# Scatter stage of a PEER encoder layer: one-hot tables made by wide instructions with eight tokens innermost

## The reference, cut to what matters

```
best, sel = lax.top_k(cand, PEER_TOPK)
idx = jnp.take_along_axis(cand_idx, sel, axis=-1)     # first key * 128 + second key
g = jax.nn.softmax(best, axis=-1).astype(h.dtype)
...
a = jax.nn.gelu(jnp.einsum('td,ted->te', xb, u)) * gb
return jnp.einsum('te,ted->td', a, exp_v[ib])
```

## Time and profile before

| what | value |
|---|---|
| median of three timed runs | 5582.73 us |
| profiled execution, its own time | 5577.84 us |
| its span, first to last instruction | 5576.1 us |
| PE / DVE / ACT / POOL busy over the span | 86% / 59% / 26% / 3% |
| mean granted TensorE clock | 0.919 of full speed |
| L1760 + L1761 + L1762 busy | 253.8 + 317.5 + 334.3 us, 1024 instructions each |

### The profile page before, as it was taken

The page is one execution under the profiler, slowest core; times in us unless marked ns, Lnnn a source line. Parts: engine busy times, 40 slices in busy tenths (PEclk is TensorE's granted clock), DMA queues, the critical chain, the costliest instruction groups (busy, mean ns, idle before and its releaser), DMA issues. The chain is left out here.

```text
span 5576.1 us, 62426 instructions
## 1 busy us (share of the span) xinstructions
PE 4798.6 (86%) x21520; PEld 3810.7 (68%) x21520; DVE 3294.1 (59%) x7335; ACT 1433.6 (26%) x1603; POOL 144.3 (3%) x96
## 2 busy tenths in 40 slices
PE   2998997959798696777767499999999999999997
PEld 1666665748576584555555388888888888888885
DVE  5666763145432598999999677644444444444445
ACT  3444442122212212333333211211221112211121
POOL 0000000010000001011110000000000000000000
PEclk9899996969898797888888799999999999999998
DMA  3000001125222101334433433322222212222222
GB/s 119 20 21 22 23 14 40 64 96 190 105 94 75 57 27 42 99 122 132 128 105 99 151 143 141 138 68 68 72 75 79 68 68 72 75 79 68 68 71 76
DMA packets 236090, 455.70 MB, mean 82 GB/s; under 512 B 12320, under 2 KB 143776, under 8 KB 232736
## 3 DMA queue, kind: packets, MB, share of 16 engines
q1 hardware_dynamic: 218656, 386.75, 20.8%
q10 hardware_dynamic: 11520, 37.75, 1.8%
q0 software_dynamic: 5760, 29.36, 1.5%
HBM read 336.38 MB, written 117.44 MB: 81 GB/s over the span
## 5 line engine op out<-in xcount | busy, mean ns | idle before, releaser
L2017 DVE TENSOR_TENSOR y<-y,psum 128x512 f32<-128x512 f32 x1024 | 679.5, 684 | 374.6 <-PE psum L375 374.4
L373 PE MATMUL psum<-act_hi,v_hi 128*128 128x512 f32 x2048 | 799.9, 391 | 55.2 <-DVE v_lo L1994 52.7
L374 PE MATMUL psum<-act_lo,v_hi 128*128 128x512 f32 x2048 | 798.3, 390 | 0.0
L375 PE MATMUL psum<-act_hi,v_lo 128*128 128x512 f32 x2048 | 798.0, 390 | 0.0
L1987 DVE SCALAR_TENSOR_TENSOR g<-g,psum 128x1024 f32<-128x1024 f32 x88 | 107.5, 1221 | 770.0 <-ACT psum L1952 770.0
L373 PE MATMUL psum<-in_hi,u_hi 128*128 128x512 f32 x1408 | 547.8, 389 | 1.9 <-DVE u_lo L1983 1.9
L374 PE MATMUL psum<-in_lo,u_hi 128*128 128x512 f32 x1408 | 547.7, 389 | 0.0
L375 PE MATMUL psum<-in_hi,u_lo 128*128 128x512 f32 x1408 | 547.7, 389 | 0.0
L373 PEld LDWEIGHTS psum<-act_hi,v_hi 128*128 128x128 f32 x2048 | 385.2, 188 | 140.1 <-issue 52.9
L1952 ACT ACTIVATE psum<-psum 128x1024 f32<-128x1024 f32 x88 | 88.7, 1008 | 1513.2 <-PE psum L375 1513.2
L375 PEld LDWEIGHTS psum<-act_hi,v_lo 128*128 128x128 f32 x2048 | 385.3, 188 | 80.4
(11 more groups left out here) (332 smaller groups left out, 8558.0 us busy)
## 6 DMA issues: line engine op xcount, KB each, us to landing
route_scratch<-sc_stage SPq DMA_DIRECT2D x32, 2048.0 KB, 10.6
g<-route_scratch SPq DMA_DIRECT2D x128, 512.0 KB, 3.3
v_raw<-peer_v_dram SPq DMA_DIRECT2D x128, 512.0 KB, 5.1
u_raw<-peer_uT_dram SPq DMA_DIRECT2D x88, 512.0 KB, 5.4
sc_u_raw<-peer_uT_dram SPq DMA_DIRECT2D x42, 512.0 KB, 5.2
hidden_scratch<-sc_gelu_t ACTq DMA_DIRECT2D x40, 512.0 KB, 4.4
u_raw<-hidden_scratch SPq DMA_DIRECT2D x40, 512.0 KB, 4.4
gates_ada<-w_adaT_dram POOLq DMA_DIRECT2D x16, 1024.0 KB, 5.6
```

Of the source, the lines that this page charges most:

```text
L373: pe.matmul(out, w_hi, x_hi, start=start, stop=False)
L374: pe.matmul(out, w_hi, x_lo, start=False, stop=False)
L375: return pe.matmul(out, w_lo, x_hi, start=False, stop=stop)
L2017: dve.tensor_tensor(to, to, ps[:, 4 + n % 4], ALU.add).then_inc(added, 1)
```

## The change

`second` stays one instruction a token and takes its key from a table of its own (`second_key`). For the first key, DVE now makes for all 8 tokens of a group at once a one-hot table `first` (one `tensor_tensor` compare over 128 x 8 = 1024 elements), and then `w_hi` and `w_lo` as products of `first` with the weight parts (one `tensor_tensor` multiply each, 1024 elements). Both inputs are float16. The layout of these three is `[selection, table, key, token]`, with the eight tokens of the group innermost; the rows of keys and weights are read with a step of 0 over the keys and a step of 1 over the tokens. DVE waits on its own `first_hot` semaphore between the compare and the products, with the 8 `second` instructions in between. `key_wide` (each key number eight times) is made once by one more POOL instruction at the stage's start. PE's list has the same matmuls in the same order, but the moving operand is now `w_hi[:, s, :, tok]`: 128 float16 values, 8 elements (16 bytes) apart, where before they were adjacent.

```diff
-                        do(dve.tensor_copy(key_pair[:].rearrange("k a t -> k (a t)"), ps[:, 4, 0:2 * P]))
+                        do(dve.tensor_copy(rows[:, 0], ps[:, 4, 0:P]))
+                        do(dve.tensor_copy(second_key[:], ps[:, 4, P:2 * P]))
                         do(dve.tensor_scalar(scaled[:], ps[:, 4, 2 * P:3 * P], WEIGHT_SCALE, None, ALU.mult))
                         all_so_far()
-                        do(dve.tensor_copy(weight_h[:], scaled[:]))
+                        do(dve.tensor_copy(rows[:, 1], scaled[:]))
                         all_so_far()
-                        do(dve.tensor_copy(parts[:, 0], weight_h[:]))
-                        do(dve.tensor_tensor(parts[:, 1], scaled[:], weight_h[:], ALU.subtract))
+                        do(dve.tensor_tensor(rows[:, 2], scaled[:], rows[:, 1], ALU.subtract))
                         all_so_far()
                         for q in range(GROUPS):
                             s = q % 2
                             dve.wait_ge(matrices, b * QUADS + (2 * q + 2))
+                            row = lambda r: rows[:, r, q * GROUP:(q + 1) * GROUP].unsqueeze(1).to_broadcast([SEL, KEYS, GROUP])
+                            dve.tensor_tensor(first[:, s], key_wide[:], row(0), ALU.is_equal).then_inc(first_hot, 1)
                             for g in range(GROUP):
                                 t = q * GROUP + g
-                                at_first, at_second = key_pair[:, 0, t:t + 1], key_pair[:, 1, t:t + 1]
-                                dve.tensor_scalar(second[:, s, g], key_of[:], at_second, None, ALU.is_equal)
-                                dve.tensor_scalar(w_hi[:, s, g], key_of[:], at_first, parts[:, 0, t:t + 1], ALU.is_equal, ALU.mult)
-                                made = dve.tensor_scalar(w_lo[:, s, g], key_of[:], at_first, parts[:, 1, t:t + 1], ALU.is_equal, ALU.mult)
+                                dve.tensor_scalar(second[:, s, g], key_of[:], second_key[:, t:t + 1], None, ALU.is_equal)
+                            dve.wait_ge(first_hot, b * GROUPS + (q + 1))
+                            dve.tensor_tensor(w_hi[:, s], first[:, s], row(1), ALU.mult)
+                            made = dve.tensor_tensor(w_lo[:, s], first[:, s], row(2), ALU.mult)
                             made.then_inc(onehots, 1)
...
-                                    pe.matmul(to, second[:, s, tok], w_hi[:, s, tok], start=True, stop=False)
-                                    last = pe.matmul(to, second[:, s, tok], w_lo[:, s, tok], start=False, stop=True)
+                                    pe.matmul(to, second[:, s, tok], w_hi[:, s, :, tok], start=True, stop=False)
+                                    last = pe.matmul(to, second[:, s, tok], w_lo[:, s, :, tok], start=False, stop=True)
```

More of the change, by code:

```diff
@@ L1569, in scatter_weights @@
         turned = self.sem("sc_turned")
+        first_hot = self.sem("sc_first_hot")
         onehots = self.sem("sc_onehots")
@@ L1591, in scatter_weights @@
             scaled = self.sb(c, "sc_scaled", [SEL, P])
-            key_pair = self.sb(c, "sc_key_pair", [SEL, 2, P])
-            weight_h = self.sb(c, "sc_weight_h", [SEL, P], F16)
-            parts = self.sb(c, "sc_weight_parts", [SEL, 2, P])
+            second_key = self.sb(c, "sc_second_key", [SEL, P])
+            rows = self.sb(c, "sc_rows_t", [SEL, 3, P], F16)
             iota16 = self.sb(c, "sc_iota16", [P, TOPK], F16)
@@ L1597, in scatter_weights @@
             second = self.sb(c, "sc_second", [SEL, 2, GROUP, KEYS], F16)
-            w_hi = self.sb(c, "sc_w_hi", [SEL, 2, GROUP, KEYS], F16)
-            w_lo = self.sb(c, "sc_w_lo", [SEL, 2, GROUP, KEYS], F16)
+            key_wide = self.sb(c, "sc_key_wide", [SEL, KEYS, GROUP], F16)
+            first = self.sb(c, "sc_first", [SEL, 2, KEYS, GROUP], F16)
+            w_hi = self.sb(c, "sc_w_hi", [SEL, 2, KEYS, GROUP], F16)
+            w_lo = self.sb(c, "sc_w_lo", [SEL, 2, KEYS, GROUP], F16)
             stage = self.sb(c, "sc_stage", [P, KEYS, P])
@@ L1660, in _ @@
                     pool.iota(key_of[:], [[1, KEYS]], base=0, channel_multiplier=0, allow_small_or_imprecise_dtypes=True).then_inc(iotas, 1)
+                    pool.iota(key_wide[:], [[1, KEYS], [0, GROUP]], base=0, channel_multiplier=0, allow_small_or_imprecise_dtypes=True).then_inc(iotas, 1)
                     pool.sem_inc(u_split, 1)
@@ L1677, in _ @@
                     dve.sem_inc(onehots, 2)
-                    dve.wait_ge(iotas, 2)
+                    dve.wait_ge(iotas, 3)
                     LINKS = 57
```

## The result

| | time of the timed runs (us) | span | clock |
|---|---|---|---|
| before | 5581.62 median of 4 | 5576.1 | 0.919 |
| changed kernel | 5671.26 median of 4 (5661.14 to 5672.51) | 5659.4 | 0.909 |

The ratio is 1.0156, 95% interval 1.0142 to 1.0170: 1.6% slower, where 3.4% faster was forecast. The profiled execution is the 5661.14 one, 83.3 us over the profiled one of before (5577.84); the three others lie near 5672, so the trace shows some 6 us less than the difference of the medians, 89.6.

A forecast was written before the change was run, and what follows sets the result against it. DVE was taken to bound the group phase, with PE and ACT following. At 16 x 3.4 + 4.1 = 58.5 us against 82.1, eight blocks save 189 us, so 5577.84 becomes 5389, plus 4.9 for the median: 5394 us, range 5350 to 5475.

The forecast's parts named there:

- PE's strided matmul: Group phase: each float16 matmul with strided moving operand taken at double cost, 0.11 us, making PE's group 3.16 us.
- The upper end of 0.22: Highest cost drawn for PE's strided matmul: four times, 0.22 us, making PE's group 4.92 us.
- rival 4: PE's strided read costs four times: 78.7 us a group phase plus 2.6 of tail, 5577 us, no change; chance 0.06.
- rival 5: PE's strided read at five times, 0.275 us: group 5.8 us, +14.2 us a block, 5696 us, slower; chance 0.09.
- the 189 us of gain: Group phase 58.5 us against 82.1: 23.6 us fewer in each of 8 blocks, 189 us in all.
- The clock: Group phase: share at the lower clock level falls by half, to 0.2, with PE nearly full; PE's group 3.4 us.
- The tail: Transposes at a block's end: PE's last group ends some 0.9 us later behind DVE; taken as nothing.
- The sum: Group phase 16 x 3.4 + 4.1 = 58.5 us, leading to a forecast time of 5394 us.
- POOL's 4.1 us of stalls: Group phase: 4.1 us a block from two DVE instructions slowed to some 2.3 us, left as they are.
- DVE's side: Group phase: three wide instructions at 0.61 us start to start, eight `second` at 0.16; group 3.12 us, 4.87 before.
- Rival 1: No penalty for PE's strided read, DVE alone sets the pace: group phase 54.0 us, 5358 us; chance 0.18.
- the question that I named as decisive: Sign of being wrong: PE's matmuls further apart than 0.2 us, or DVE's compare alone over 1.1 us.

The follow-up runs named there:

- run 1: Changed kernel with PE reading 128 adjacent values of the same tables instead of values 8 elements apart (routing placed wrongly): 5350.41 us, ratio 0.9587.
- run 2: Kernel before, narrow table instructions kept, with PE's moving operand read at a step of 8 elements (routing placed wrongly): 5689.22 us, ratio 1.0190.
- INNER 4: Changed kernel with tables in two halves of four tokens, so PE reads at a step of 4; all computation done: 5357.04 us, ratio 0.9602.
- run 4: Changed kernel with PE's moving operand read at a step of 2 elements (routing placed wrongly): 5346.95 us, ratio 0.9580.
- run 9: Changed kernel with tables in four quarters of two tokens, so PE reads at a step of 2; all computation done: 5350.28 us, ratio 0.9588.
- run 7: Changed kernel with scatter matmul operands exchanged: strided tables stationary, adjacent second-key table moving (routing placed wrongly): 5347.12 us, ratio 0.9585.
- run 3: Changed kernel with PE's moving operand read at a step of 4 elements (routing placed wrongly): 5357.57 us, ratio 0.9602.
- run 6: Changed kernel with PE's moving operands read from a constant tile at steps of 6 and 3 elements (routing values wrong): one execution, 5381.30 us.
- run 5: Changed kernel with PE's moving operands read from a constant tile at steps of 16 and 8 elements (routing values wrong): one execution, 5683.35 us.
- run 8: The same run as INNER 4: changed kernel with tables in two halves of four tokens, all computation done: 5357.04 us, ratio 0.9602.

## Why the prediction was wrong

**The step that failed** is the term of PE's strided matmul. I took 0.11 us, double, from ACT's strided write; it is 0.228, 4.1 times 0.055. The row was the nearest there was, but of another engine and the other direction. The upper end of 0.22 was drawn; it was within 4% of the truth, and I gave what lay there (rivals 4 and 5) 0.15 of the chance and left it outside the range. The Trainium skill's page Advanced Engine Details and Errata (SBUF Cachelines) says that a new line for each access is penalised, which agrees with the changed kernel; that two hits on a line are enough, which it says too, doesn't (step 4: 0.115). What the Trainium skill's page SBUF — State Buffer (Door 1: The DMA port swizzle) says, that 8 elements of bf16 may be stepped over for free, is contradicted by runs 1 and 2 for PE's moving operand (0.062 us at a step of 1, 0.228 at 8).

With 0.228 in the forecast's own sum and the upper clock throughout, a group is 1.40 + 3.65 = 5.05 us, a phase 80.8, and 83.4 with rival 4's 2.6 us of tail: 10 us more than before in eight blocks, 5593. So this term alone turns the 189 us of gain into nothing. It doesn't give the 5671.

**The clock** failed as well, and gives most of what is left. I expected the share at the lower level to fall by half with PE busy; over the eight group phases the mean clock went from 0.80 to 0.76, with PE busy 61% of the time before and 95% after. In run 1 it rose to 0.92, with PE busy 75%. And in the changed kernel it is low where it costs. Four stretches in order of time, of wide matmuls, strided, wide, strided (clock in the third column from the end):

```profile
2306.60:2308.00 1.40, 1.40 (x4) 1.09 (x4) 1.40 (x3) 1.40 (x3) 1.13 (x1) 0.50 0.00 0
2309.20:2311.90 2.70, 2.70 (x13) 1.39 (x12) 2.30 (x9) 1.08 (x1) 0.07 (x1) 1.00 0.51 143
2312.50:2314.00 1.50, 1.50 (x5) 1.14 (x4) 1.50 (x8) 0.95 (x1) 0.00 (x0) 0.50 0.00 0
2317.00:2318.00 1.00, 1.00 (x6) 0.56 (x5) 0.00 (x0) 0.82 (x1) 0.00 (x0) 1.00 0.00 0
```

Over all groups the mean clock is 0.61 while PE runs the six wide matmuls and 0.82 while it runs the sixteen strided ones; in run 1 it is 0.94 over the wide ones. The strided matmuls take 0.227 us at either level, so an upper clock is of no use to them; the wide ones take 0.233 and 0.43, and came to 38.4 us a block where 96 x 0.233 would be 22.4. A group takes PE (55.3 + 38.4) / 16 = 5.86 us, against 5.05 at the upper clock and 6.17 at the lower: 0.81 us more in each of 128 groups, 104 us. That is more than the 78 between 5593 and 5671, since the blocks' idle time at their end became 20 us shorter. Why the clock falls in the one kind of stretch and comes back in the other wasn't tried. The result is near rival 5's 5696, and its 5.8 us a group nearly hit, but by luck: it has five times the cost of the read, and the truth is four times and a lower clock.

**The tail** at the transposes was taken as nothing (rival 4 had 2.6 us). In the seven blocks after the first, DVE waits there 9.7 us a block, where it waited 1.5. The forecast added PE's groups up as if DVE's tables took as long. They don't: from its first table to its last DVE took 87.3 us on average (84.8 to 88.7), 82.2 before, while PE's 16 groups take 93.8. DVE makes the last tables before PE has done the groups ahead of them, and the rest of PE's time shows as this wait: 87.3 + 9.7 = 97.0, which is the 3.1 of the first tables and PE's 93.8. By DVE's path a block grew by 5.1 us in the tables and 8.2 in the wait; it lost 2.5 of idle time at its end and 1.1 in the selection. That is 9.7 of the 10.2.

**The sum** was off on its own too. A step of 4 costs 0.115 us, which is nearly the 0.11 that I took, and the kernel that has it (INNER 4, all of the work done) takes 5357 us and not 5394. PE's group there is (28.4 + 25.9) / 16 = 3.39 us, the 3.4 of the forecast. But DVE's tables take 55.2 us a block and not 58.5: I had added POOL's 4.1 us of stalls to a phase that PE was to bound, which rival 4 doesn't do. And I had left out the shorter idle time at a block's end, 20 us in eight blocks.

**What held.** DVE's side to the hundredth: 688 ns for a product (0.69 taken), the compare at the same rate (709 with POOL's stalls in it), `second` 0.16 to 0.17 apart, a group of 3.1 us, no cost of the `first_hot` wait. The rows of one group of the changed kernel:

```profile
2517.55 0.69 DVE L1761 TENSOR_TENSOR sc_first<-sc_key_wide,sc_rows_t 128x1024 f16<-128x1024 f16 x1 [1.82 <-PE psum L1857]
2518.16 1.39 DVE L1764 TENSOR_SCALAR sc_second<-sc_key_of,sc_second_key 128x128 f16<-128x128 f16 x8
2519.46 0.69 DVE L1766 TENSOR_TENSOR sc_w_hi<-sc_first,sc_rows_t 128x1024 f16<-128x1024 f16 x1
2520.06 0.69 DVE L1767 TENSOR_TENSOR sc_w_lo<-sc_first,sc_rows_t 128x1024 f16<-128x1024 f16 x1
2521.55 2.29 DVE L1698 TENSOR_TENSOR sc_cand<-top_vals 128x2048 f32 x1 [0.80 <-DVE sc_w_lo L1767]
```

Rival 1, DVE alone setting the pace, said 5358; with a step of 1 or 2 runs 1, 4 and 9 measured 5350, 5347 and 5350. Part of this closeness is luck: DVE's tables take 55.2 us a block in run 1 and not 54.0, and the shorter idle time makes up for it. And the question that I named as decisive, the distance of PE's matmuls at more than 0.2 us, is the one that decided.

## What to carry to other kernels

A layout has a writer and a reader: when the writer's instructions are made wide by putting another index innermost, price the reader's step first, above all if the reader is to become the bound. Where the trace has no row for that step, its cost must keep its full range in the forecast, since here a factor of two would have been a gain and one of four was none. A mean clock over a phase hides on which instructions the low level falls: ask which of them it slows. Here the writer needed only a run of two elements to keep its rate, and that left the reader nearly adjacent; in another kernel the shortest such run is worth trying first.

## What the runs showed of the hardware

- PE's moving operand, 128 float16 columns, from start to start against the step in elements, middle values at the upper clock: 1: 0.056 us, 2: 0.058, 3: 0.103, 4: 0.116, 6: 0.157, 8: 0.227, 16: 0.232. At the lower clock: 1 and 2: 0.107, 4: 0.116, 8: 0.227. So steps of 1 and 2 follow the clock, and steps of 4 and 8 don't.
- The stationary operand with a step of 8: 148 ns a load against 103, hidden behind the matmuls (run 7).
- DVE's float16 product (`tensor_tensor`) of 1024 elements keeps 0.68 to 0.69 us with runs of 8, 4 or 2 elements inside, the second input repeated over the keys (688, 682, 679 ns).
- The mean granted clock of the group phases doesn't follow the share of time in which PE's records show it busy, nor whether its reads are strided: 0.80 at 61% (before), 0.92 at 75% (run 1), 0.95 at 90% (run 3, step 4), 0.96 at 92% (run 6, steps 6 and 3), 0.76 at 95% (changed kernel), 0.74 at 93% (run 2, step 8), 0.72 at 96% (run 5, steps 16 and 8). What sets it wasn't tried.
- DVE's 3.3 us of idle time at each block's end shrank to 0.80 us in the changed kernel, whose DVE list has 13 instructions fewer a group. It is 0.80 in runs 1, 3, 8 and 9, which have that list, and 3.3 in run 2, which has the list of before and PE's slow reads: so it goes with DVE's list and not with PE's pace. That wasn't foreseen and is worth up to 20 us in eight blocks; its cause wasn't tried.
